# Layer 1's w_ada tiles on VectorE during the feed-forward, and RWKV's triangular inverse in compact 64x64 blocks

## What is computed

```python
def _rwkv_scan(r, w, kk, a, v, kt, s0):          # 4 heads of 64, two directions, two streams of 128 tokens
    def step(S, xs):
        sk = jnp.einsum('bhvk,bhk->bhv', S, kk_t)
        S = S * w_t[:, :, None, :] - sk[..., None] * (a_t * kk_t)[:, :, None, :] + v_t[..., :, None] * k_t[..., None, :]
        return S, jnp.einsum('bhvk,bhk->bhv', S, r_t)
...
def _trunk(x, cvec, P, caches):
    for l in range(DEPTH):                       # DEPTH = 2
        mod = (jax.nn.silu(cvec) @ P['w_ada'][l] + P['b_ada'][l])[:, None, :]
        sh1, sc1, g1, sh2, sc2, g2 = jnp.split(mod, 6, axis=-1)
        mix, ctx_tensors = _token_mixer(x * (1.0 + sc1) + sh1, P, l, ctx)
        x = _layer_norm(DN_ALPHA * x + g1 * mix, P['ln1_g'][l], P['ln1_b'][l])
        h = x * (1.0 + sc2) + sh2
        f = _dense_ffn(h, P, l // 2) if l % 2 == 0 else _moe_ffn(h, P, l // 2)
        x = _layer_norm(DN_ALPHA * x + g2 * f, P['ln2_g'][l], P['ln2_b'][l])
```

## Time and profile before

| | |
|---|---|
| median of 3 runs | 2020.51 us |
| profiled execution, its own time | 2018.66 us |
| its span (first to last instruction) | 2016.8 us |
| TensorE matmul busy | 1928.9 us, 96% of the span |
| VectorE busy | 452.2 us, 22% |
| ScalarE busy | 247.2 us, 12% |
| DMA, mean of 16 engines (q1) | 63.5% of the span |

### The profile page before, as it was taken

One profiled execution on the slowest core, in us unless ns is written; L12 is line 12 of the kernel. 1 busy time (PEld: TensorE's weight loads), 2 busy tenths in 40 slices (PEclk: granted clock), 3 DMA queues, 4 the chain that ended last, 5 costly groups with the idle time before them and its releaser, 6 DMA issues.

```text
span 2016.8 us, 27907 instructions
## 1 busy us (share of the span) xinstructions
PE 1928.9 (96%) x12228; PEld 1493.3 (74%) x12228; DVE 452.2 (22%) x950; ACT 247.2 (12%) x507; POOL 11.6 (1%) x24
## 2 busy tenths in 40 slices
PE   6999999999999989989997999999999999999996
PEld 4877678887888877888887766676666666688753
DVE  1243424122000133454434100000111000200103
ACT  0121112102000023122203000000000000000001
POOL 0000000000000000000000000000000000000000
PEclk8999999999999999999998999999999999999999
DMA  9336663414343342300311999999999999998794
GB/s 392 137 144 256 236 243 128 145 63 167 128 185 125 146 169 105 105 24 22 126 64 60 421 421 421 421 421 421 420 421 421 421 421 421 421 332 303 268 422 173
DMA packets 73719, 511.11 MB, mean 253 GB/s; under 512 B 9346, under 2 KB 10818, under 8 KB 12036
## 3 DMA queue, kind: packets, MB, share of 16 engines
q1 hardware_dynamic: 72964, 508.76, 63.5%
q0 software_dynamic: 640, 0.66, 0.1%
HBM read 507.68 MB, written 1.70 MB: 253 GB/s over the span
## 4 chain that ended last, share of the span: by engine, by line
PE 54%; DMA 6%; DVE 1%; ACT 0%; issue 0%; SPq 0%; ACTq 0%; DVEq 0%
PE bank L591 22%; PE bank L1081 9%; PE bank L1095 7%; DMA area<-in_moe 6%; PE bank L1105 5%; PE bank L942 2%; PE bank L807 1%; PE bank L792 1%; PE bank L1116 1%; PE bank L965 1%; PE bank L770 0%; PE bank L797 0%; PE bank L922 0%; PE bank L1088 0%; DVE area L1517 0%
## 5 line engine op out<-in xcount | busy, mean ns | idle before, releaser
L591 PE MATMUL bank<-hT,area 128*128 128x256 f32 (+1 forms) x2080 | 463.6, 383 | 6.2 <-DVE hT L1522 5.9
L591 PEld LDWEIGHTS bank<-hT,area 128*128 128x128 f32 (+1 forms) x2080 | 394.7, 191 | 70.6 <-issue 12.6
L591 PEld LDWEIGHTS bank<-mixer,area 128*128 128x128 f32 x2720 | 312.3, 192 | 21.5 <-issue 19.9
L591 PE MATMUL bank<-mixer,area 128*128 128x128 f32 x2720 | 315.3, 275 | 2.4 <-DVE mixer L1739 1.4
L1081 PE MATMUL bank<-area,mixer 128*64 128x256 f32 x2240 | 252.7, 380 | 7.0 <-DMA area<-in_moe 7.0
L1081 PEld LDWEIGHTS bank<-area,mixer 128*64 128x64 f32 x2240 | 163.3, 137 | 100.9 <-issue 32.3
L1517 DVE TENSOR_TENSOR hT<-hT,bank 128x256 f32<-128x256 f32 x154 | 64.8, 421 | 715.8 <-ACT hT L1450 577.3
L1095 PE MATMUL bank<-area,hT 128*128 128x512 f32 x336 | 153.8, 601 | 0.0
L1105 PE MATMUL bank<-area,hT 128*64 128x512 f32 x560 | 127.6, 597 | 2.7 <-DMA area<-in_moe 2.2
L1095 PEld LDWEIGHTS bank<-area,hT 128*128 128x128 f32 x336 | 60.5, 190 | 71.5 <-issue 71.5
L604 PE MATMUL bank<-area,cS 128*32 128x256 f32 x768 | 91.4, 394 | 15.5 <-DMA area<-in_ada 15.5
(11 more groups left out here) (295 smaller groups left out, 1361.5 us busy)
## 6 DMA issues: line engine op xcount, KB each, us to landing
area<-in_moe SPq DMA_DIRECT2D x336, 1024.0 KB, 25.6
area<-in_mix SPq DMA_DIRECT2D x62, 1024.0 KB, 4.8
area<-in_ada SPq DMA_DIRECT2D x48, 1024.0 KB, 6.8
area<-in_dense SPq DMA_DIRECT2D x33, 1024.0 KB, 6.7
cst<-in_cst SPq DMA_DIRECT2D x1, 2121.5 KB, 19.5
xT<-in_xT SPq DMA_DIRECT2D x1, 1024.0 KB, 16.1
out_yT<-xT SPq DMA_DIRECT2D x4, 256.0 KB, 2.5
mixer<-in_wbB SPq DMA_DIRECT2D x2, 256.0 KB
```

Of the source, the lines that this page charges most:

```text
L591: last = mm(out, a, b, start=(n == 0), stop=(n == len(pairs) - 1), **kw)
```

## The change

Two things change.

First, layer 1's 24 tiles of `w_ada` leave TensorE. `early_pair` is called for 8 pairs only, no longer within the levels. Three further buffers of 1 MB (`late_w`) are filled by DMAs issued between those of the dense units. VectorE multiplies each tile by silu(c) during the dense loop: for 8 row chunks and 2 streams one multiply-add over 128x256, 16 instructions a tile, 384 in all (`late_products`). The sums over the 128 partitions remain: TensorE takes them with matmuls whose moving operand is one column of ones (`late_rows`): 4 for each tile. 19 tiles are summed between the last two `down`, one within and four behind the matmuls of the layer norm that follows. SP's and VectorE's dense loops are written out instead of looped.

Second, the inverse stops at blocks of 64 (`LEVELS` = 5). The two diagonal 64x64 blocks of a head lie in the two halves of the partitions, so `Tm`, `TmT`, `P` are 128x256 instead of 128x512, and each 128x128 matmul becomes two 64x64 ones, in opposite corners of the array (`HALVES`). The transpose becomes a matmul with the identity. The block off the diagonal is handled at the end by substitution: from the half solution, 4 matmuls with M's off-diagonal block, a copy to `Ws` on VectorE, 4 matmuls with `TmT`, and a second copy to `nU` on ScalarE, for each d.

```diff
-LEVELS = 6
+LEVELS = 5
+H = P // 2
+HALVES = [slice(0, H), slice(H, P)]
...
-EARLY = [f"ada{n}" for n in range(ADA_FIRST, L * ADA_TILES)]
+EARLY = [f"ada{n}" for n in range(ADA_FIRST, ADA_TILES)]
+
+LATE_SLOTS = 3
+LATE_OF_UNIT = [[2 * u + 2, 2 * u + 3] for u in range(DENSE_UNITS - 3)] + [[18, 19, 20], [21, 22, 23], []]
+LATE_START = [0, 1]
+LATE_FIRST, LATE_MID = 8, 19
...
+            def late_load(t):
+                if t >= LATE_SLOTS:
+                    sp.wait_ge(sem("late_used"), t - LATE_SLOTS + 1)
+                else:
+                    sp.wait_ge(sem("merged_ready"), 4)
+                sp.dma_start(late_w[t % LATE_SLOTS], ins["ada"][1, t].rearrange("p (c n) -> p c n", c=KC))\
+                    .then_inc(sem(f"full{RING + t % LATE_SLOTS}"), 16)
...
-            dense_loop(sp, dense_unit)
+            for t in range(LATE_SLOTS):
+                late_load(t)
+            for u in range(DENSE_UNITS):
+                unit_loads("dense", None if u < 2 else u, u % 2, dense[:, :, u],
+                           [2 * u - 1, 2 * u] if u >= 2 else [])
+            for t in range(2 * DENSE_UNITS - 1, ADA_TILES):
+                late_load(t)
...
                         for h in range(4):
-                            last = mm(bk(2 + 3 * d, 4, P)[:, h, :], MTQ[d][:, h // 2, 0, h % 2, :], Tm[d][:, h, :],
-                                      start=True, stop=True)
+                            for x in HALVES:
+                                last = mm(bk(2 + 3 * d, 4, H)[x, h, :], MTQ[d][x, h // 2, 0, h % 2, x], Tm[d][x, h, :],
+                                          start=True, stop=True)
                         last.then_inc(sem(f"inv_MT{d}"), 1)
                         if j > 1:
                             for h in range(4):
-                                last = nc.tensor.transpose(bk(4 + 3 * d, 4, P)[:, h, :], Tm[d][:, h, :], ident)
+                                for x in HALVES:
+                                    last = mm(bk(4 + 3 * d, 4, H)[x, h, :], Tm[d][x, h, :], ident[x, x],
+                                              start=True, stop=True)
                             last.then_inc(sem("inv_turned"), 1)
-                    if l == 0:
-                        early_pair()
...
                 if st == 1 and l == 0:
                     early_pair()
+                n = k * (LEVELS + 1)
+                for d in range(2):
+                    one, two = HALVES[d], HALVES[1 - d]
+                    pe.wait_ge(sem("nu_half"), 2 * (k - 1) + d + 1)
+                    for h in range(4):
+                        last = mm(bk(6 + d, 4, H)[two, h, :], MTQ[d][one, h // 2, 0, h % 2, two],
+                                  nU[d][one, 64 * h:64 * h + 64], start=True, stop=True)
+                    last.then_inc(sem(f"inv_MT{d}"), 1)
+                for d in range(2):
+                    two = HALVES[1 - d]
+                    pe.wait_ge(sem(f"inv_P{d}"), n)
+                    for h in range(4):
+                        last = mm(bk(4 + d, 4, H)[two, h, :], TmT[d][two, h, :], Ws[d][two, h, :],
+                                  start=False, stop=True, skip_group_check=True)
+                    last.then_inc(sem(f"inv_TP{d}"), 1)
                 pe.wait_ge(sem("nu_ready"), 2 * k)
...
+            def late_rows(t0, t1):
+                for t in range(t0, t1):
+                    pe.wait_ge(sem("late_used"), t + 1)
+                    cols = bank[3 if t < LATE_FIRST else 2][:, 4 * t:4 * t + 4].rearrange("p (h s) -> p h s", h=2)
+                    for st in range(2):
+                        for h in range(2):
+                            last = mm(cols[:, h, st:st + 1], late_sum[t][:, 256 * st + P * h:256 * st + P * h + P],
+                                      C("ones")[:, 0:1], start=True, stop=True)
+                    if t + 1 in (LATE_FIRST, ADA_TILES):
+                        last.then_inc(sem("ada_turned"), 1)
...
+                pe.wait_ge(sem("dense_hid"), DENSE_UNITS - 1)
+                late_rows(0, LATE_MID)
                 down(0, (DENSE_UNITS + 1) // 2, DENSE_UNITS, final=True)
...
+            def late_products(t):
+                dve.wait_ge(sem(f"full{RING + t % LATE_SLOTS}"), 16 * (t // LATE_SLOTS + 1))
+                w, total = late_w[t % LATE_SLOTS], shaped(late_sum[t], (2, TW))
+                for c in range(KC):
+                    for st in range(2):
+                        if c > 0:
+                            dve.wait_ge(sem("dve_chain"), steps[0] - 1)
+                            last = v.scalar_tensor_tensor(total[:, st, :], w[:, c, :], cS[:, c, st:st + 1],
+                                                          total[:, st, :], ALU.mult, ALU.add)
+                        else:
+                            last = scaled(total[:, st, :], w[:, c, :], cS[:, c, st:st + 1])
...
+                last.then_inc(sem("late_used"), 1)
...
                 if l == 0:
-                    dense_loop(dve, dense_hidden)
+                    for t in LATE_START:
+                        late_products(t)
+                    for u in range(DENSE_UNITS):
+                        dense_hidden(0, u, u, u % 2, u < 2)
+                        for t in LATE_OF_UNIT[u]:
+                            late_products(t)
+                    dve.wait_ge(sem("ada_turned"), ADA_TILES // 4 + 1)
+                    take_modulations(1, 0, 16, bank[3])
+                    fuse_modulations(1)
                     layer_norm(1)
```

More of the change, by code:

```diff
@@ L227, in build_program @@
         shared = 1024 * 5
-        Tm, TmT = [cut(4, P) for _ in range(2)], [cut(4, P) for _ in range(2)]
+        Tm = [cut(4, H) for _ in range(2)]
+        cut(4, P)
+        TmT = [cut(4, H) for _ in range(2)]
+        Ws = [cut(4, H) for _ in range(2)]
         Xs, nU = [cut(256) for _ in range(2)], [cut(256) for _ in range(2)]
@@ L236, in build_program @@
         K2n = P1
+        Pm = [shaped(qT[:, 2 * d, :], (4, H)) for d in range(2)]
         cut = carver(work, WORK)
@@ L256, in build_program @@
         merged, mtmp, yLN, rstd = cut(KC, TOK), cut(KC, TOK), cut(KC, TOK), cut(TOK)
+        cut = carver(wide, WIDE)
+        late_w = [cut(KC, TW) for _ in range(LATE_SLOTS)]
+        late_sum = [mixer[:, 512 * t:512 * t + 512] for t in range(14)]
+        late_sum += [wide[:, LATE_SLOTS * SLOT + 512 * t:LATE_SLOTS * SLOT + 512 * t + 512] for t in range(6)]
+        late_sum += [work[:, 6400 + 512 * t:6912 + 512 * t] for t in range(4)]
         cut = carver(work, WORK)
@@ L822, in rwkv_stream @@
                     for h in range(4):
-                        last = mm(bank[4 + d][:, 64 * h:64 * h + 64], TmT[d][:, h, :], Xs[d][:, 64 * h:64 * h + 64],
-                                  start=True, stop=True)
+                        for x in HALVES:
+                            last = mm(bk(4 + d, 4, H)[x, h, :], TmT[d][x, h, :], Xs[d][x, 64 * h:64 * h + 64],
+                                      start=(h == 0), stop=False, skip_group_check=True)
                     last.then_inc(sem("u_done"), 1)
@@ L1561, in _ @@
             dve.wait_ge(sem("ada_turned"), ADA_FIRST // 4)
[L1562 removed]
+            take_modulations(0, 0, 16, bank[1])
             v.memset(zeros[:, 0:1], 0.0).then_inc(sem("mod_read"), 1)
@@ L1736, in rwkv_stream @@
                     last.then_inc(sem("k2_ready"), 1)
+                for d in range(2):
+                    two = HALVES[1 - d]
+                    dve.wait_ge(sem(f"inv_MT{d}"), k * (LEVELS + 1))
+                    v.tensor_copy(Ws[d][two], bk(6 + d, 4, H)[two]).then_inc(sem(f"inv_P{d}"), 1)
+                if st == 0:
                     dve.wait_ge(sem("k2T_done"), l + 1)
```

115 lines of the change are left out of this document (67 added, 48 removed).

## The result

The changed kernel takes 1961.09 us (median of 4 runs, 1955.74 to 1967.0) where the kernel before takes 2020.62 (4 runs): a ratio of 0.971 with a 95% interval of 0.9677 to 0.9742. Its profiled execution took 1955.74 us. Run again later, beside 8 runs of the kernel before (2019.69), it takes 1958.87 us, ratio 0.9701 [0.968, 0.9723]. The forecast was 1954, against the profiled executions 2018.66 - 64.6; measured is 2018.66 - 62.9. That execution is the fastest of its four; the medians lie 7 and 5 us above the forecast, inside its range. The closeness of the total is in part luck: the levels gained 8 us more than forecast, the sums and what stands behind them cost 17 us more, and 6.5 us of the measured gain come from places that the change doesn't touch. The rest of this document takes these apart.

What follows compares the result with a forecast made beforehand. TensorE was taken as the bound, its matmuls filling 96% of the span. From the profiled 2018.66 us: - 47.7 + 16.7 - 3 - 29.6 - 1 = 1954.1, forecast 1954 us, range 1939 to 1996.

Steps and rivals of the forecast that it cites:

- 12 pairs and 6 turns leave: Layer 0's levels: w_ada work leaving TensorE saves its whole time, taken from the windows: -47.7 us.
- four streams of levels: Levels of the inverse: 448 small matmuls at 0.037 us plus 0.9 waiting, 17.5 us, 9.3 less in each stream.
- right-hand side and substitution: Solution after the levels: chain grows from 2.43 to 4.3 us, +1.85 in three streams, +2.1 in layer 0's second.
- VectorE's preparation: Preparing Tm and TmT gets some 0.5 us shorter for each d; TensorE waits for it in layer 0 alone: -1 us.
- 152 column sums: Ahead of the last down: 19 tiles' single-column instructions on TensorE at 0.110 us each, +16.7 us.
- layer norm and projection: Matmuls fill the 3.81 us wait, so the clock holds for the 80 matmuls behind it: -3 us.
- products on VectorE, DMA: Dense stretch: 384 multiply-adds at 475 ns fit in VectorE's room, DMA share rises to about 0.63; no cost.
- The step that chose 0.037: Levels: spacing of 64x64 matmuls if two corners overlap, 0.029 us by arithmetic plus 0.008.
- Rival (c): TensorE's clock falls to 1.2 GHz in the levels and single-column sums: slower, 2027 us; chance 0.07.
- The bound of -3.3: Layer norm: the larger bound on the gain from a held clock in the 80 matmuls behind it.
- (a): Levels: corners take turns or issue floor is 0.059 us, so the second part costs +8.6: 1992 us; chance 0.27.

Runs made afterwards that it cites:

- part 1 alone: Kernel before with only layer 1's w_ada moved to VectorE, the inverse left at 6 levels of 128x128: 2002.72 us, ratio 0.9912.
- mixed kernel: Changed kernel with the 76 single-column matmuls ahead of the last down laid between the matmuls of the last two downs: 1948.73 us, ratio 0.9658.
- strips: Changed kernel with partition sums taken four tiles at once in 32-column strips of the array, products moving, then copied and turned: 1939.44 us, ratio 0.9609.
- strips_hid: As strips, but VectorE forms the last unit's hid ahead of the products of tiles 21 to 23: 1938.39 us, ratio 0.9604.

## Why the prediction came out right, point by point

The terms of the sum, profiled execution against profiled execution:

| term | forecast, us | measured, us | from |
|---|---|---|---|
| 12 pairs and 6 turns leave | -47.7 | -47.5 | levels of part 1 alone |
| four streams of levels | -37.2 | -45.4 | windows: 26.95, 26.95, 26.84, 26.83 to 16.63, 15.02, 15.02, 15.53 |
| right-hand side and substitution | +7.7 | +7.3 | end of the levels to the output, four streams |
| VectorE's preparation | -1 | -1.6 | layer 0's two streams, 0.8 each |
| 152 column sums | +16.7 | +28.7 | 628.52 to 657.25 |
| last down at a low clock | 0 | +3.0 | 9.9 against 6.9 |
| layer norm and projection | -3 | -1.0 | start of L1035 to the end of the 80 |
| products on VectorE, DMA | 0 | 0 | dense stretch 222.15 in both |
| ahead of layer 0's first stream | 0 | -1.6 | start of L770, 141.29, to that of L807, 139.67 |
| layer 1, outside the terms above | 0 | -4.9 | see below |
| sum (rounded) | -64.6 | -62.9 | |

**The levels, mis-sized by 8.2 us.** The step that chose 0.037 added to a quarter of the full pace the 0.008 by which L690's rows exceed half of it. The corners need no such addition: 0.029, the bare arithmetic. That makes 448 x 0.029 = 13.0 us; the rest of the 15.02 is 2.0 us (of which TensorE is idle 0.5), where 0.9 was forecast. The Trainium skill, TensorEngine Tiling (Array Packing), Gotcha 1: PSUM Pressure, says that tiles in different rows of the array cannot access one PSUM bank at the same time, and I had weighed that against the overlap. It did not hold here: the two corners write two halves of one bank and overlap at 0.029 us, and making them take turns costs 14 to 16 us. The measurement decides. The Trainium skill, TensorE: Matmul & The Clock Gate, Back-to-back issue gap, puts the issue floor near 25 ns; the 0.029 of this trace lies above it and doesn't contradict it.

**The substitution and the preparation, right to about 1 us.** The chain from L864 to L895 is 4.03 us where 4.3 was forecast: +1.6, not +1.85, in three streams, and +2.1 in layer 0's second, as forecast; the right-hand side ahead of it adds 0.4 in all. `Tm`'s matmuls take 0.46 us instead of 0.6 (L813, L775), VectorE's last piece 0.76 instead of 1.41. From the first L807 to the first level it is 14.90 us where it was 15.71, in both of layer 0's streams; in layer 1's first, 18.85 against 18.86, so nothing.

**The sums, mis-sized by 12 us, and the step that went wrong.** The 0.110 us was read from 8 instructions of L751, which stand alone between wide ones at a clock of 1.00. The duration was right, and the mixed kernel shows it again. What I didn't ask is whether the clock would stay with 152 in a row. Rival (c) had that mechanism for levels and sums together at 0.07; it occurred for the sums alone, and the levels, 448 small matmuls in 15 us, kept 1.00. The same fall cost 3 us in the last down.

**The layer norm, mis-sized by 2 us, for two reasons.** I had tied the clock to waiting only; single-column matmuls fill the wait, but they don't hold the clock. And the 17.3 us that I took for the 80 projections at full clock leave out the waits for pieces of `hT`: with 128 columns moving the clock did hold, and they took 18.57. The bound of -3.3 was out of reach; a held clock gives -1.7.

**6.5 us that no term of the forecast has; by the traces nearly all of it is chance.** Layer 0's first stream starts 1.6 us earlier than in the kernel before; when the changed kernel is run again, it starts 2.5 us later than in the first trace (L807 at 142.19 instead of 139.67). In layer 1 the trace of before has short falls of the clock in projections that the change doesn't touch, and the trace after has not. The first of these projections in four traces: before, after, strips, and strips_hid, which has the same code as strips from well ahead of this place on:

```profile
801.03 8.85 PE L591 MATMUL bank<-area,hT 128*128 128x256 f32 x32
...
762.71 7.17 PE L626 MATMUL bank<-area,hT 128*128 128x256 f32 x32
...
743.44 7.17 PE L627 MATMUL bank<-area,hT 128*128 128x256 f32 x32
...
742.11 8.86 PE L627 MATMUL bank<-area,hT 128*128 128x256 f32 x32
```

In both of the last two TensorE is busy for the whole of the 22 us ahead of it, at a clock of 1.00. Two more such places are 7.50 against 7.17 us (895.92, 844.90; 7.86 when the changed kernel is run again) and 8.59 against 7.17 (951.73, 890.67; 8.62 with strips). Around the three places stand 1.7, 1.1 and 1.4 of the 4.9 us; a part of the 1.1 is the smaller L813, the other 0.7 is spread. Why the clock falls there in one trace and not in another, no run here shows. Without these 6.5 us the profiled execution would have come out near 1962, where the median is (1961.09). So the error of the terms that I did forecast is +8, not +1.7.

**VectorE and the DMAs, right.** 479 ns against 475, hid never late, the new loads at a share of 0.62 against 0.63. The margin was larger than thought, since 14 products start only 0.40 us apart.

Two numbers of the rivals don't come out of their own terms, and neither enters the forecast: 0.115 us for a small matmul gives 2094 to 2095, not 2097, and the +1 in (a) has no source.

## What to carry to other kernels

Price a new run of instructions by the row of one such instruction only after asking what the clock will be when there are many in a row: here 152 single-column matmuls took 28.7 us, the same ones spread between wide matmuls 16.7 (152 x 0.110), and with 128 columns moving 17.0. Before a total that came out right is believed, compare pieces that the change doesn't touch in both traces: here they hold 6.5 of the 62.9 us. Work that is moved off a full engine is worth its whole time there, and the engine that takes it is free until its own work for one period exceeds the period: 12.2 + 1.4 us fitted into 20.7, 26.7 + 1.4 didn't. And an experiment that changes values may change how much work the program does, so compare the counts of the groups before its total.

## What the runs showed of the hardware that was not expected

- Back-to-back single-column fp32 matmuls with 128x128 weights let the granted clock fall from 1.00 to 0.50 with TensorE busy all the time and waiting for nothing; 0.110 us each became 0.189 in the mean of the run. With 128 columns moving they take 0.112 and the clock stays.
- 64x64 matmuls in opposite corners of the array, writing two halves of the partitions of one bank, overlap: 0.029 us each, with the clock at 1.00.
- With the corners in sequence the pace over a stream's levels is 0.041: within one corner it is 0.06, and groups of different corners overlap at their borders.
- VectorE's multiply-add of 128x256 lasts 479 ns. Where each waits for the one before the last, they start 0.40 us apart (14 in 5.62 us). With each product twice, every second one waits for the last: the starts are then 0.52 and 0.40 us apart in turn (446.65, 447.17, 447.57), 28 in 12.91 us.
- The granted clock can fall behind 22 us in which TensorE was busy without a wait, in one trace (strips_hid) and not in another (strips) with the same code there: 32 projections in 8.86 us or in 7.17.
